# Last expert stage: both activation halves behind one 512-column matmul, the sides added on VectorE, second products one block later

## What is computed

```python
u_sel = expert_u[idx]
act = jax.nn.gelu(jnp.einsum('td,tkd->tk', xb, u_sel).astype(jnp.float32))
coeff = (gate * act).astype(xb.dtype)
return jnp.einsum('tk,tkd->td', coeff, expert_v[idx])
```

## Time and profile before

| | us |
|---|---|
| median of 3 runs | 2200.14 |
| lowest, highest | 2198.88, 2202.81 |
| the profiled execution | 2200.17 |
| its span, first to last instruction | 2198.4 |
| TensorE busy in the span | 2106.0 |
| VectorE busy | 1533.8 |
| ScalarE busy | 985.8 |
| GpSimd busy | 803.9 |

### The profile page before, as it was taken

The page is one execution under the profiler, slowest core; times in us unless marked ns, Lnnn a source line. Parts: engine busy times, 40 slices in busy tenths (PEclk is TensorE's granted clock), DMA queues, the critical chain, the costliest instruction groups (busy, mean ns, idle before and its releaser), DMA issues.

```text
span 2198.4 us, 45771 instructions
## 1 busy us (share of the span) xinstructions
PE 2106.0 (96%) x14382; PEld 1957.3 (89%) x14382; DVE 1533.8 (70%) x3212; ACT 985.8 (45%) x1367; POOL 803.9 (37%) x322
## 2 busy tenths in 40 slices
PE   6799999999999999999988999998999999999997
PEld 5799799999998888899978998998999988888997
DVE  1543319998888888777735531599899788887776
ACT  2554444544543333344445444445545433333443
POOL 3488678910000000144354986698000000003442
PEclk8799999999999999999999999999999999999999
DMA  6345447654457777755453554576554587776553
GB/s 174 128 145 184 150 150 227 201 179 159 158 177 236 241 241 241 220 182 190 163 178 112 176 185 146 168 228 190 160 166 163 192 241 243 241 241 198 185 187 124
DMA packets 155042, 410.72 MB, mean 187 GB/s; under 512 B 17331, under 2 KB 67668, under 8 KB 154924
## 3 DMA queue, kind: packets, MB, share of 16 engines
q1 hardware_dynamic: 154220, 407.75, 57.7%
q0 software_dynamic: 704, 1.57, 0.6%
HBM read 382.00 MB, written 27.26 MB: 186 GB/s over the span
## 4 chain that ended last, share of the span: by engine, by line
PE 75%; DVE 15%; issue 7%; DMA 2%; ACT 0%; SPq 0%; DVEq 0%; ACTq 0%; POOLq 0%
PE bank L1043 36%; PE bank L1241 31%; PE bank L1293 5%; DMA rel_scratch<-act 2%; DVE area L921 2%; DVE area L924 2%; DVE area L881 2%; DVE area L901 1%; DVE area L878 1%; DVE area L793 1%; DVE area L898 1%; DVE area L926 1%; DVE area L885 1%; DMA ring<-in_stream 1%; DVE area L890 1%
## 5 line engine op out<-in xcount | busy, mean ns | idle before, releaser
L440 POOL TENSOR_TENSOR halves<-ring,halves 128x1024 fp32r<-128x1024 f32 x308 | 797.7, 2604 | 1357.6 <-ACT halves L505 1356.1
L1043 PE MATMUL bank<-hT,halves 128*128 128x256 f32 x8688 | 1125.8, 286 | 24.4 <-POOL halves L440 11.4
L505 ACT ACTIVATE halves<-ring 128x1024 fp32r<-128x1024 f32 x668 | 707.4, 1060 | 925.8 <-PE bank L1043 467.0
L1043 PEld LDWEIGHTS bank<-hT,halves 128*128 128x128 f32 x8688 | 1071.8, 192 | 34.6 <-issue 11.2
L1241 PE MATMUL bank<-halves,coef 128*128 128x512 f32 x3072 | 713.2, 391 | 3.9 <-DVE coef L977 3.9
L1241 PEld LDWEIGHTS bank<-halves,coef 128*128 128x128 f32 x3072 | 574.5, 189 | 123.0 <-DVE coef L977 5.9
L938 DVE TENSOR_TENSOR halves<-ring,halves 128x1024 fp32r<-128x1024 f32 x360 | 438.6, 1219 | 39.2 <-issue 22.1
L971 DVE TENSOR_TENSOR act<-act,area 128x256 f32<-128x256 f32 x256 | 223.7, 874 | 100.3 <-ACT act L615 95.4
L951 DVE TENSOR_SCALAR onehot<-ids,x 128x128 f32<-128x128 f32 x512 | 172.9, 338 | 1.9 <-issue 1.9
L1293 PE MATMUL bank<-onehot,x 128*128 128x128 f32 x1024 | 156.2, 274 | 0.0
L950 DVE TENSOR_SCALAR x<-ids,x 128x128 f32<-128x128 f32 x512 | 142.4, 278 | 18.2 <-PE bank L1293 17.1
(11 more groups left out here) (136 smaller groups left out, 973.0 us busy)
## 6 DMA issues: line engine op xcount, KB each, us to landing
ring<-in_stream SPq DMA_DIRECT2D x672, 512.0 KB, 3.5
held_blocks<-act SPq DMA_DIRECT2D x188, 128.0 KB, 1.9
act<-held_blocks SPq DMA_DIRECT2D x188, 128.0 KB, 3.1
area<-rel_scratch SPq DMA_DIRECT2D x2, 1024.0 KB, 6.6
rel_scratch<-act POOLq DMA_DIRECT2D x1, 1532.0 KB, 35.7
area<-in_consts SPq DMA_DIRECT2D x2, 576.0 KB, 3.8
x<-in_x SPq DMA_DIRECT2D x1, 1024.0 KB, 5.0
out_y<-x SPq DMA_DIRECT2D x2, 512.0 KB, 2.7
```

The lines of the kernel that those rows point to most:

```text
L440: pool.tensor_tensor(halves[:, s, 1, :], ring[:, s, :], halves[:, s, 0, :].bitcast(F32), ALU.subtract)\
L505: a.activation(halves[:, s, 0, :], ring[:, s, :], ACT.Copy).then_inc(hi_done, 1)
L1043: i = pe.matmul(o, stationary[a], moving[b], start=begin and n == 0, stop=end and n == len(TERMS) - 1)
```

## The change

In the last stage a first product is made of 16 matmuls in place of 24. The high weights of a chunk meet both activation halves in one matmul of 512 columns, whose left 256 columns collect high x high and whose right 256 collect high x low; the low weights meet the high activations in a matmul of 256 columns that adds to the left side. VectorE then adds the two sides with a `tensor_reduce` from PSUM into `act` (semaphore `summed`), and ScalarE's GELU works on `act` in place. TensorE's order becomes u0 u1 u2 v0 u3 v1 u4 v2 ... u31 v29 v30 v31. The tile order in DRAM, SP's waits and the roles of the ring slots follow that order. GpSimd makes the low halves of the first three positions (u0, u1, u2) in a row; VectorE's first tile of the stage is position 3.

```diff
+                for p in range(3):
+                    low(T_MU + p, p, l)
+                with pool.Fori(1, MAIN // 2 - 1) as r:
+                    low(r * 4 + T_MU, 0, l)
+                    low(r * 4 + (T_MU + 2), 2, l)
+                low(NT - 4, 0, l)
...
-                        a.wait_ge(coef_ready, l * NK + block - 1)
-                        gelu(k)
+                        a.wait_ge(summed, l * MAIN + block + (1 - EARLY))
+                        a.activation(act[:, k, :], act[:, k, :], ACT.Gelu_apprx_tanh).then_inc(act_done, 1)
...
-                gated(EARLY, 0, T_MU + 2, 2, T_MU - 1)
-                gated(EARLY + 1, 1, T_MU + 4, 0, T_MU)
+                def add_halves(j, p, k):
+                    v.wait_ge(coef_ready, l * NK + j + (EARLY - 1))
+                    v.wait_ge(tiles_used, l * NT + p + (T_MU + 1))
+                    v.tensor_reduce(act[:, k, :], bank_u[k][:, :].rearrange("p (c t) -> p t c", c=2), AX.X, ALU.add)\
+                        .then_inc(summed, 1)
+                add_halves(0, 0, 0)
+                add_halves(1, 1, 1)
+                gated(EARLY, 0, T_MU + 3, 3, T_MU - 1)
+                add_halves(2, 2, 0)
+                gated(EARLY + 1, 1, T_MU + 5, 1, T_MU)
                 with v.Fori(1, MAIN // 2 - 1) as r:
                     for k in range(2):
-                        gated(r * 2 + (EARLY + k), k, r * 4 + (T_MU + 2 + 2 * k), (2, 0)[k], r * 4 + (T_MU - 1 + 2 * k))
+                        add_halves(r * 2 + (1 + k), r * 4 + 2 * k, 1 - k)
+                        gated(r * 2 + (EARLY + k), k, r * 4 + (T_MU + 3 + 2 * k), (3, 1)[k], r * 4 + (T_MU + 2 * k))
+                add_halves(MAIN - 1, 2 * MAIN - 4, 1)
...
                 def u_main(b, s, k):
                     pe.wait_ge(lo_pool, l * LOP + b + (T_HU - EARLY + 2))
-                    pe.wait_ge(act_done, l * NK + b - 1)
-                    u_product(s, k)
+                    w = halves[:, s].rearrange("p h (k c) -> p h k c", k=KD)
+                    for c in range(KD):
+                        pe.matmul(bank_u[k][:, :], w[:, 0, c], hT[:, :, c], start=c == 0, stop=True, skip_group_check=True)
+                        i = pe.matmul(bank_u[k][:, 0:S], w[:, 1, c], hT[:, 0, c], start=False, stop=True,
+                                      skip_group_check=True)
+                    i.then_inc(tiles_used, 1)
...
+                u_next(EARLY + 2, 2, 0)
+                v_product(EARLY, 3, 0)
+                with pe.Fori(1, MAIN // 2 - 1) as r:
+                    u_next(r * 2 + (EARLY + 1), 0, 1)
+                    v_product(r * 2 + (EARLY - 1), 1, 1)
+                    u_next(r * 2 + (EARLY + 2), 2, 0)
+                    v_product(r * 2 + EARLY, 3, 0)
+                u_next(NK - 1, 0, 1)
+                v_product(NK - 3, 1, 1)
                 v_product(NK - 2, 2, 0)
                 v_product(NK - 1, 3, 1)
```

More of the change, by code:

```diff
@@ L310, in program @@
         act_done = sem("act_done")
+        summed = sem("summed")
         held_stored = [sem(f"held_stored{i}") for i in range(2)]
@@ L406, in _ @@
                 for s in range(RING):
-                    if s in (0, 1, 3):
-                        sp.wait_ge(lo_pool, l * LOP + (T_HU + 1 + (1, 2, 0, 3)[s]))
+                    if s < 3:
+                        sp.wait_ge(lo_pool, l * LOP + (T_HU + 2 + s))
                     else:
@@ L413, in _ @@
                     for s in range(RING):
-                        if s % 2:
-                            sp.wait_ge(lo_pool, l * LOP + r * 2 + (T_HU + 1 + (s - 1) // 2))
+                        if s % 2 == 0:
+                            sp.wait_ge(lo_pool, l * LOP + r * 2 + (T_HU + 1 + s // 2))
                         else:
@@ L674, in _, with main @@
                         high(r * RING + (T_PV + RING + s), s)
-                def main(p, s, block=None, last=False):
+                def main(p, s, block=None, k=0, last=False):
                     a.wait_ge(tiles_used, l * NT + p + (T_MU + 1))
@@ L682, in main @@
                     if block is not None:
-                        k = 1 if s == 1 else 0
-                        a.wait_ge(coef_ready, l * NK + block - 1)
-                        gelu(k)
[L688 to L698, removed]
+                        a.wait_ge(summed, l * MAIN + block + (1 - EARLY))
+                        a.activation(act[:, k, :], act[:, k, :], ACT.Gelu_apprx_tanh).then_inc(act_done, 1)
+                main(0, 0, EARLY, 0)
+                main(1, 1, EARLY + 1, 1)
+                main(2, 2, EARLY + 2, 0)
+                main(3, 3)
+                with a.Fori(1, MAIN // 2 - 1) as r:
+                    main(r * 4, 0, r * 2 + (EARLY + 1), 1)
+                    main(r * 4 + 1, 1)
+                    main(r * 4 + 2, 2, r * 2 + (EARLY + 2), 0)
+                    main(r * 4 + 3, 3)
+                main(2 * MAIN - 4, 0, NK - 1, 1, last=True)
             roots(NSCAL * DEPTH, lambda i: a.wait_ge(x_ready, 4 * DEPTH + (i + 1)))
@@ L986, in _ @@
                         gated(b, s % 2, b + T_PV, s, b + (T_PV - 1), block=r * RING + (s - 2))
-                gated(EARLY, 0, T_MU + 2, 2, T_MU - 1)
-                gated(EARLY + 1, 1, T_MU + 4, 0, T_MU)
+                def add_halves(j, p, k):
[8 more added lines that the diff above has]
+                gated(EARLY + 1, 1, T_MU + 5, 1, T_MU)
                 with v.Fori(1, MAIN // 2 - 1) as r:
                     for k in range(2):
-                        gated(r * 2 + (EARLY + k), k, r * 4 + (T_MU + 2 + 2 * k), (2, 0)[k], r * 4 + (T_MU - 1 + 2 * k))
-                gated(NK - 2, 0, NT - 2, 2, NT - 5)
-                gated(NK - 1, 1, NT - 1, 3, NT - 3)
+                        add_halves(r * 2 + (1 + k), r * 4 + 2 * k, 1 - k)
+                        gated(r * 2 + (EARLY + k), k, r * 4 + (T_MU + 3 + 2 * k), (3, 1)[k], r * 4 + (T_MU + 2 * k))
+                add_halves(MAIN - 1, 2 * MAIN - 4, 1)
+                gated(NK - 2, 0, NT - 2, 2, NT - 4)
+                gated(NK - 1, 1, NT - 1, 3, NT - 2)
                 v.wait_ge(tiles_used, l * NT + NT)
@@ L1307, in u_main, with u_next @@
                     pe.wait_ge(lo_pool, l * LOP + b + (T_HU - EARLY + 2))
-                    pe.wait_ge(act_done, l * NK + b - 1)
-                    u_product(s, k)
[L1312 to L1318, removed]
+                    w = halves[:, s].rearrange("p h (k c) -> p h k c", k=KD)
[4 more added lines that the diff above has]
+                    i.then_inc(tiles_used, 1)
+                def u_next(b, s, k):
+                    pe.wait_ge(summed, l * MAIN + b - (EARLY + 1))
+                    u_main(b, s, k)
+                for j in range(2):
+                    pe.wait_ge(act_done, l * NK + (EARLY + j - 1))
+                    u_main(EARLY + j, j, j)
+                u_next(EARLY + 2, 2, 0)
[7 more added lines that the diff above has]
+                v_product(NK - 3, 1, 1)
                 v_product(NK - 2, 2, 0)
@@ L1393, in lay_out @@
         o[T_PV + 2:T_MU] = v[:EARLY - 2]
[L1394 to L1397, removed]
+        o[T_MU:T_MU + 2] = u[EARLY:EARLY + 2]
+        o[T_MU + 2:NT - 3:2] = u[EARLY + 2:]
+        o[T_MU + 3:NT - 1:2] = v[EARLY:-2]
+        o[NT - 2:] = v[-2:]
     return out.reshape(DEPTH * NT, P, TILE)
```

## The result

| | before | after |
|---|---|---|
| median of 10 runs each, us | 2200.34 (2198.58 to 2202.81) | 2205.77 (2204.22 to 2207.09) |
| profiled span, us | 2198.4 | 2203.2 |

The changed kernel takes 1.0025 of the time of the one before, 95% interval 1.0016 to 1.0035: 5.4 us slower. Forecast were 2204.8 us (+4.6) and "slower by over 0.2%" as the likeliest of the three. Total and sign were right. Of the seven terms four were right in mechanism and size, the one of the clock only as a mean of two unlike layers; two were mis-sized, in the steady part, and their errors, of opposite sign, hid each other in part. The experiments found that, and a version that is faster than both kernels.

A forecast was written before the change was run, and what follows sets the result against it. TensorE was taken to bound the steady part, so only its savings or new waits count. The terms summed to +2.3 us a layer, +4.6 for two layers, on 2200.17 us: 2204.8 us, range 2197 to 2212.

The forecast's parts named there:

- slower by over 0.2%: Whole kernel: slower than 2204.5 us, chance 0.48, against 0.41 for within and 0.11 for faster.
- First products: TensorE, last stage: eight pairs of 512 and 256 columns take 2.79 us instead of 2.87, -2.6 us a layer.
- The reduce: VectorE's new reduce from PSUM takes 0.69 us, with nothing added for the strided read.
- The steady wait: VectorE's chain behind u(j+1) takes 5.64 us against TensorE's 5.54, biting every second block: +1.4 us a layer.
- The entry: Stage entry: GpSimd's third low half goes ahead of the subtract, so v(95) starts late, +2.1 us a layer.
- The clock: After 4.0 us idle at the entry the granted clock falls again, costing something more than before: +0.4 us a layer.
- v0: First second product of the stage: waits 0.60 us for VectorE where it waited 0.22, +0.4 us a layer.
- The end: End of the stage: only v29 stands ahead of v30, 2.75 us against VectorE's 3.39, +0.6 us a layer.
- Rival (a): Stage entry: GpSimd's third low half does not get ahead of the subtract; 2199.8 us, no measurable change; chance 0.22.
- (b): TensorE: the 512-column form is cheaper than its row, -8.6 instead of -2.6 us a layer; 2192 us; chance 0.08.
- (c): VectorE becomes the bound: the strided reduce costs 1.22 us, deciding from about 1.1; 2222 us; chance 0.10.

The follow-up runs named there:

- e3: The changed kernel with VectorE's low half of v(j) put ahead of the reduce of u(j+1): 2205.26 us, ratio 1.0026 to the kernel before.
- e1: The changed kernel with GpSimd's third low half held back until the coefficients of v(95) are ready: 2198.38 us, ratio 0.9999 to the kernel before.
- e6: The changed kernel with a 64-column copy and a wait for it ahead of each reduce: 2213.72 us, ratio 1.0067 to the kernel before.
- e8: The changed kernel with each 512-column matmul split into two of 256: 2206.86 us, ratio 1.0038 to the kernel before.
- e9: e4 with a first product's eight 512-column matmuls first, then its eight of 256: 2187.18 us, ratio 0.9946 to the kernel before.
- e5: The kernel before with GpSimd's low halves at the entry held until the coefficients of v(95) are ready: 2190.74 us, ratio 0.9968 to the kernel before.
- e2: The changed kernel with all three GpSimd low halves at the entry held until v(95)'s coefficients are ready: 2193.14 us, ratio 0.9973 to the kernel before.
- e4: The changed kernel with the edits of e2 and e3 together: 2189.35 us, ratio 0.9956 to the kernel before.
- e7: e4 with each 512-column matmul split into two of 256: 2194.4 us, ratio 0.9974 to the kernel before.

## Why the prediction held, point by point

1. **First products, -2.6 a layer: mis-sized.** The step that failed is the price of a pair as 229.2 + 119.6 ns, taken from a second product made of 512s alone and a first product made of 256s alone. Neither row has the two lengths in turn. In turn they cost 352 ns, and the second product behind them 0.03 more. The steady part saves 0.03 a block. The term's size can be read from e3, where no wait of the steady part is left: its layer 2 is 187.43 - 186.58 = +0.85 us against before; less the 2.01 of the entry, and with the 0.22 at v0 that e3 no longer has, -0.9 a layer remain for the first products. The written bound "0, if a moving operand in two runs gives the 10 ns a pair back" had the size, for another reason.
2. **The reduce, 0.69 us, unheld: right**, 692 ns over 64, with the stride in PSUM free.
3. **The steady wait, +1.4: mechanism and chain right, term mis-sized.** The chain is 5.65 (5.64 forecast), but what it is late against is 5.59, not 5.54. It adds 0.01 to 0.02 a block (5.61 against 5.59), +0.2 to +0.4 a layer. Terms 1 and 3 hang on the same number, so an error in it gives half of itself back: together -0.5 and -0.7 came in the two layers, where -1.2 was forecast.
4. **The entry, +2.1: right**, 2.01 in both layers, by the mechanism named; e1 shows it by taking it away. (The sum for GpSimd's turn gives 2.26 us and not 2.24, which changes nothing here.) Rival (a), "GpSimd's third low half does not get ahead", is out.
5. **The clock, +0.4: right as a mean, by luck.** 1.1 and 0.0, with the same wait of 3.9 us ahead, and no mechanism was given that would tell the two apart. The traces show when the clock fell. Eight such waits of 3.94 or 3.95 us are on record (both layers of after, e3, e6 and e8). In four the clock had fallen before v(95) started, and v(95) took 5.30 to 5.49 us; in four it fell within v(95), which took 4.34 to 4.62. What decides which of the two comes stays open.
6. **v0, +0.4: right**, +0.50. The 0.1 more is the low half of VectorE, 1.32 for 1.22, where it met the end of GpSimd's at 2017.45.
7. **The end, +0.6: right**, +0.61.

The stages came to +6.1 and not +4.6: 1.2 from terms 1 and 3, 0.3 from the clock, 0.2 from v0, -0.2 from the entry. The rest of the span was 1.3 shorter in this execution than in that of before; by the medians of ten runs the whole is +5.4. That the total lands within 1 us of 2204.8 is partly luck: term 1 was off by +1.7 a layer and term 3 by -1.1. A gain of 0.02 us a block in place of 0.08 would have given about 2207 by the same sum, and the total does not tell the two apart; the 2.81 us of a first product do. Rivals (b) and (c) needed another pair price and a reduce of 1.1 us; neither came. (b) is partly what e9 shows to be possible: not a cheaper 512, but the same matmuls in another order.

**What the change is worth.** e5 against e9 is the fair comparison, each with the entry mended: 182.76 and 179.23, 3.5 us a layer for the change with grouped matmuls and the low half ahead of the reduce. As written, with the entry mended (e2), it loses 0.46 a layer. Half of what e9 gains over before in the stages, 7.6 of 14.7 us, comes from the wait on GpSimd, which has nothing to do with the change.

## What to carry to other kernels

Before an engine is given work ahead of need, look at who shares its access to memory at that moment: low halves of GpSimd that nobody wanted yet cost TensorE a wait and its clock, and one wait on a semaphore gave 3.8 us a layer back. Take the price of a matmul from a row with the same neighbours, and where lengths are mixed, group them. Where a chain and TensorE's pace are within 0.1 us and a late start pushes the next one, as here, a saving on either alone is worth half, so free the chain first and then measure the pace by itself.

## What the runs showed of the hardware

- **Mixed lengths.** float32r matmuls, each with a new weight tile: 512 and 256 columns in turn 352 ns a pair and +0.03 us on the second product behind; grouped 226 + 119 = 345 ns and nothing behind (e4, e9). I had expected the order to be free.
- **A waiting instruction of GpSimd gets in at each gap.** After, VectorE had three instructions held in a row, 2.62, 2.26 and 2.44 us against 0.42, 0.29 and 0.42 in e2; the reduce from PSUM is at 0.69 beside GpSimd (2016.60 after).
- **The clock after equal waits.** 3.95 us idle ahead of v(95) in layer 1 and 3.94 in layer 2 cost 1.1 and 0.0 us more than the 1.93 us of before did: the granted clock fell within the wait in the one, after v(95) had started in the other. No idle time, no loss (e2). Elsewhere in the program the granted clock differed between kernels with the same code there (0.83 against 1.00 in the windows of e3 and e2), and the rest of their spans by 5 us. In one kernel too: the shortest execution of e7, 2187.3 us, had a mean granted clock of 0.985, the longest, 2197.1, one of 0.981. Comparing by stage took that out.
